# Two inversions half a period apart in a recurrent stage, and their products as 32x32 tiles

## The chip, the cores and the metric

One Trainium2 chip, one of its cores. The metric is device time in microseconds (us) of one execution, lower is better. The kernel before took 2627.87 us (median of 3 runs, 2627.56 to 2632.1).

## The reference, cut to what matters

Two transformer-like layers on one sequence of 1024 tokens, width 1024, all float32: an attention and convolution layer with an MLP, then a hybrid layer whose second half is a recurrent mixer (eight heads of 64). Only that mixer is touched. With a state of 64x64 per head it computes, token by token:

```
def rwkv7_step(state, inp):
    r_t, w_t, k_t, v_t, kk_t, a_t = inp
    sa = jnp.einsum('bhvk,bhk->bhv', state, -kk_t)
    state = (state * w_t[:, :, None, :] + sa[..., None] * (kk_t * a_t)[:, :, None, :]
             + v_t[..., None] * k_t[:, :, None, :])
    y = jnp.einsum('bhvk,bhk->bhv', state, r_t)
    return state, y
...
    _, y = lax.scan(rwkv7_step, s0, (tm(rh), tm(wh), tm(kh), tm(vh), tm(kk), tm(ah)))
```

After it come a group norm over each head, a bonus term, a gate, an output projection of 1024x1024 and a final RMS norm.

## The kernel before, in words

The kernel runs through five phases; the recurrent stage is the first part of the last one (`rwkv_phase`). Each engine has its own instruction stream, written out by hand in a loop over chunks; semaphores order the engines, and within an engine instructions start in program order.

The 1024 tokens are cut into C = 16 chunks of 64. Within a chunk the recurrence is a triangular system per head: u = (I - N)^-1 z, with N strictly triangular of 64x64. Eight heads lie as 4 pairs: head pair m in the free dimension, head e of the pair in partitions 64e to 64e+63. So one product over all heads is 8 matmuls of 64x64 (`pairs`), on two diagonal tiles of the array; a float32 matmul leaves two MATMUL and two LDWEIGHTS records.

For every chunk c:
- ScalarE takes exponentials (`exps`, L2989 to L2991), GpSimd scales the operands (`operands`, L2997 to L3004), TensorE makes the raw scores (`raw`, L3013), VectorE masks them (`masked`, L3026), ScalarE copies the two halves into one tile (`both_heads`, L3031, L3032), GpSimd multiplies it by six level masks (`chunk_levels`, L3038).
- The inverse is built in six levels: level l joins diagonal blocks of 2^l into blocks of 2^(l+1). T and G (the inverse and its transpose) start as identity plus the first mask (L3605, L3609). At each further level TensorE makes X = off_l^T T (`inv_x`), ScalarE copies X out of PSUM (L3479), TensorE makes G^T X and X^T G (`inv_w`), VectorE adds them to T (L3617) and G (L3620). The last level makes the one for G alone. Work is split into two groups of two head pairs, each with PSUM banks and semaphores of its own, so that one group's eviction lies beside the other group's product. All of these products are recorded at L3270.
- Around it: `turn` transposes k and v of the chunk (L3283, L3288; ScalarE evicts, L3465, L3467), `value_part` (L3262) multiplies values with scores (VectorE copies, L3611), `state_part` (L3262) reads the carried state, VectorE adds both (`combine`, L3585), `solve` (L3262) applies G, ScalarE copies u (L3471), `y_part` (L3343, L3347) makes the outputs, `state_product` (L3355) the update, and VectorE's `next_state` (L3590, L3591) forms the next state.

The order on TensorE in iteration c: `state_part(c-1)`, `inv_x(c, 0)`, `turn(c)`, `solve(c-1)`, `inv_x(c, 1)`, `value_part(c)`, `inv_w(c, 1)`, then levels 2 to 5 of chunk c one after the other, with `y_part(c-1)` and `state_product(c-1)` after the second x, `raw(c+1)` after the third. In chunks 8 to 12 sums of the group norm (L3188) are put between, and VectorE and ScalarE do the norm of the first half of the sequence; in chunks 11 to 15 casts for the output projection. After the last chunk TensorE makes 16 output tiles with 24 matmuls each (`project`, L425); tile 0 is made in the last iteration.

Buffers: operands `ra` three deep, scores two deep, level masks two deep; `bkt`, `uv`, `zv` two deep. Weights of the projection are loaded by SyncE into a ring of three slots; all three are full before the stage.

Of the kernel before, what the change touches and what calls it, by code (L numbers as in the profile page):

```python
# [2599 lines left out]
LEVELS = 6  # L2600
GN_EPS = 64e-5
# [10 lines left out]
def gates_phase(k):  # L2612
# [43 lines left out]
    def _(sp):  # L2656
# [19 lines left out]
        load_weights(k, sp, START["wout", 0] + RING)  # L2676
# [282 lines left out]
def chunk_buffers(k):  # L2959
# [12 lines left out]
    b.ra = [x.rearrange("p (c d) -> p c d", c=4) for x in (view_cp(k, 2560), low(0, 4 * P), low(512, 4 * P))]  # L2972
    bk, er, ek = four_of(low(1024, 2, 4 * P)), four_of(low(2048, 2, 4 * CHUNK)), four_of(low(2560, 2, 4 * CHUNK))
    b.bk = lambda c: bk[:, c % 2] if c else early(512, P)
    b.er = lambda c: er[:, c % 2] if c else early(0, CHUNK)
    b.ek = lambda c: ek[:, c % 2] if c else early(256, CHUNK)
    mm, mab = low(3072, 4, 4 * P).rearrange("p (a b) (c d) -> p a b c d", a=2, c=4), four_of(low(5120, 2, 4 * CHUNK))
    free_at = [k.later_pieces.hi_at(k.later_pieces.of_tile[2 * len(IN3_TILES) - 4 + i][0]) for i in range(2)]
    b.mm = lambda c: mm[:, c % 2] if c else four_of(k.data(free_at[0], 2, 4 * P))
    b.mab = lambda c: mab[:, c % 2] if c else four_of(k.data(free_at[1], 1, 4 * CHUNK))[:, 0]  # L2980
    b.off = k.view(XT_AT + 4096, 2 * LEVELS, 4 * CHUNK).rearrange("p (a b) (c d) -> p a b c d", a=2, c=4)
    b.mask, b.level = k.view(CP_AT + CD["mask"][0], P), k.view(CP_AT + CD["level"][0], LEVELS, CHUNK)
    b.last_er, b.er_neg = k.view(CP_AT + 2140, 4, 4), k.data(17408, 4, CHUNK)
# [3 lines left out]
def chunk_exps(k, a, b, c):  # L2987
    at = slice(c * CHUNK, (c + 1) * CHUNK)
    a.activation(b.last_er[:, c % 4], b.L[:, :, (c + 1) * CHUNK - 1], ACT.Exp, scale=-DECAY)  # L2989
    a.activation(b.er(c), b.L[:, :, at], ACT.Exp, scale=-DECAY)  # L2990
    a.activation(b.ek(c), b.L[:, :, at], ACT.Exp, scale=DECAY).then_inc(k.exp_ready, 1)  # L2991


def chunk_operands(k, g, b, c):
    at, o = slice(c * CHUNK, (c + 1) * CHUNK), b.ra[c % 3]
# [12 lines left out]
def chunk_raw(k, pe, b, c):  # L3008
    pe.wait_ge(k.ops_ready, c + 1)
    for m in range(4):  # L3010
        for e in range(2):
            half = slice(64 * e, 64 * e + 64)
            last = pe.matmul(k.bank(e if c else 4 + e).rearrange("p (m c) -> p m c", m=4)[:, m], b.bk(c)[half, m],  # L3013
                             b.ra[c % 3][half, m], start=True, stop=True)
    last.then_inc(k.raw_mm, 1)
# [6 lines left out]
def chunk_masked(k, v, b, c):  # L3022
    v.wait_ge(k.raw_mm, c + 1)
    for e in range(2):
        raw = k.bank(e if c else 4 + e).rearrange("p (m c) -> p m c", m=4)
        v.tensor_tensor(b.mm(c)[:, e], raw, over_pairs(b.mask), ALU.mult).then_inc(k.mm_ready, 1)  # L3026
# [8 lines left out]
def chunk_levels(k, g, b, c, levels=range(LEVELS)):  # L3035
# [5 lines left out]
def rwkv_phase(k):  # L3041
# [22 lines left out]
    mm = chunk.mm  # L3064
    bkt, uv, zv = four_of(low(5632, 2, 4 * P)), four_of(low(6656, 2, 4 * P)), four_of(low(7680, 2, 4 * CHUNK))
    off, tt = chunk.off, four_of(high(3072, 1, 4 * CHUNK))
    gg, zz = four_of(high(3328, 2, 4 * CHUNK)), four_of(high(3840, 1, 4 * CHUNK))
# [15 lines left out]
    x_bank, w_bank, G = (2, 4), (3, 7), (slice(0, 2), slice(2, 4))  # L3083
# [43 lines left out]
    first_split = {(12, 2): 4, (13, 2): 5, (14, 1): 6, (14, 2): 7, (14, 4): 0, (15, 1): 1, (15, 2): 2, (15, 4): 3}  # L3127
# [13 lines left out]
    def half(b, at):  # L3141
        return k.bank(b)[:, at:at + 2 * CHUNK].rearrange("p (m c) -> p m c", m=2)
# [9 lines left out]
    def _(sp):  # L3152
# [17 lines left out]
        sp.wait_ge(y_mm, C)  # L3170
        sp.dma_start(gate[1], part("gate_keep", 1)).then_inc(gate_in[1], 16)
# [12 lines left out]
    def _(pe):  # L3184
# [5 lines left out]
        def mean(i):  # L3190
            if i < 4:
                pe.wait_ge(y_read, 8)
                pe.wait_ge(s_ready, 8 + i)
# [6 lines left out]
        def variance(i):  # L3200
            pe.wait_ge(q2_ready, i + 1)
            if i < 4:
                pe.wait_ge(mm_ready, 2 * (11 + i))
# [61 lines left out]
        def group_pairs(i, bank, at, lhs, rhs):  # L3265

            out = k.bank(bank)[:, at:at + 2 * CHUNK].rearrange("p (m c) -> p m c", m=2)
            for m in range(2):
                for e in range(2):
                    last = pe.matmul(out[rows(e), m], lhs(2 * i + m, e), rhs(2 * i + m, e), start=True, stop=True)  # L3270
            return last

        def raw(c):
            pe.wait_ge(zv_ready, c)
            pe.wait_ge(turn_read, 2 * c)
            chunk_raw(k, pe, chunk, c)

        def turn(c):
            pe.wait_ge(mm_ready, 2 * c + 2)
# [16 lines left out]
        def inv_x(c, l):  # L3296

            pe.wait_ge(off_ready, LEVELS * c + l + 1)
            for i in range(2):
                if l == 0:  # L3300
                    last = group_pairs(i, x_bank[i], 0, lambda m, e: off[rows(e), c % 2, 0, m],
                                       lambda m, e: eye[rows(e)])
                else:
                    pe.wait_ge(t_ready[i], (LEVELS - 1) * c + l)
                    last = group_pairs(i, x_bank[i], 0, lambda m, e: off[rows(e), c % 2, l, m],
                                       lambda m, e: tt[rows(e), 0, m])
                last.then_inc(x_mm[i], 1)

        def inv_w(c, l):

            for i in range(2):
                pe.wait_ge(x_ready[i], (LEVELS - 1) * c + l)
                pe.wait_ge(g_ready[i], LEVELS * c + l)
                if l < LEVELS - 1:
                    group_pairs(i, w_bank[i], 0, lambda m, e: gg[rows(e), c % 2, m],
                                lambda m, e: xx[rows(e), l % 2, m])
                group_pairs(i, w_bank[i], 2 * CHUNK, lambda m, e: xx[rows(e), l % 2, m],
                            lambda m, e: gg[rows(e), c % 2, m]).then_inc(w_mm[i], 1)

        def state_part(c):  # L3320
            if c >= 1:
                pe.wait_ge(s_ready, c)
            if 8 <= c < 12:
                pe.wait_ge(d_ready, c - 7)
            pairs(5, lambda m, e: ra[c % 3][rows(e), m, 64:128], lambda m, e: st[rows(e), 0, m]).then_inc(zs_mm, 1)

        def solve(c):
            pe.wait_ge(z_ready, c + 1)
            for i in range(2):
                pe.wait_ge(g_ready[i], LEVELS * (c + 1))  # L3330
# [6 lines left out]
            pairs(6, lambda m, e: gg[rows(e), c % 2, m], lambda m, e: zz[rows(e), 0, m]).then_inc(u_mm, 1)  # L3337

        def y_part(c):
            pe.wait_ge(u_ready, 2 * c + 2)  # L3340
            for m in range(4):
                for e in range(2):
                    pe.matmul(four(6)[rows(e), m], st[rows(e), 0, m], ra[c % 3][rows(e), m, 0:64], start=m == 0,  # L3343
# [7 lines left out]
        def state_product(c):  # L3351
            pe.wait_ge(z_ready, c + 1)
            for m in range(4):
# [5 lines left out]
        for c in range(C + 1):  # L3359
            if c >= 1:  # L3360
                state_part(c - 1)
            if c < C:
                inv_x(c, 0)
                turn(c)
            else:
                project(0, (0, 4))
            if c >= 1:
                solve(c - 1)
            if c < C:
                inv_x(c, 1)  # L3370
                value_part(c)
                inv_w(c, 1)
            if c == C:
                project(0, (4, KT))
                y_part(c - 1)
            if c < C:
                for l in range(2, LEVELS):
                    inv_x(c, l)
                    if l == 2 and c >= 1:
                        y_part(c - 1)  # L3380
                        state_product(c - 1)
                    if l == 3 and c + 1 < C:
                        raw(c + 1)
                    inv_w(c, l)
                    if l == 3 and 8 <= c < 12:
                        mean(c - 8)
                    if l == 3 and 9 <= c < 13:
                        bonus(c - 9)
                    if l == 4 and 9 <= c < 13:
                        variance(c - 9)  # L3390
        for n in range(1, 16):
            project(n)
# [13 lines left out]
    def _(a):  # L3406
# [37 lines left out]
        def exps(c):  # L3444
            if c >= 2:
                a.wait_ge(ops_ready, c - 1)
            if c >= 4:
                a.wait_ge(s_ready, c - 3)
            chunk_exps(k, a, chunk, c)

        def both_heads(c):

            if c >= 2:
                a.wait_ge(off_ready, LEVELS * (c - 1))
            chunk_heads(k, a, chunk, c)

        cast_at = {(11, 5): 4, (12, 5): 5, (13, 2): 6, (13, 5): 7, (14, 2): 0, (14, 4): 1, (14, 5): 2, (15, 2): 3}
        a.wait_ge(k.in3.filled, 2 * len(IN3_TILES))
        exps(1)
        for c in range(C + 1):  # L3460
            if c < C:
                a.wait_ge(turn_mm, 2 * c + 1)
                if c >= 2:
                    a.wait_ge(y_mm, c - 1)
                a.copy(bkt[:, c % 2], four(0, P)).then_inc(turn_read, 1)  # L3465
                a.wait_ge(turn_mm, 2 * c + 2)
                a.copy(uv[64:128, c % 2], four(1, P)[64:128]).then_inc(turn_read, 1)  # L3467
            if c >= 1:
                a.wait_ge(u_mm, c)
                for e in range(2):  # L3470
                    a.copy(uv[0:64, (c - 1) % 2, :, rows(e)], four(6)[rows(e)]).then_inc(u_ready, 1)  # L3471
            if c < C:
                for l in range(1, LEVELS):
                    n = (LEVELS - 1) * c + l
                    for i in range(2):
                        a.wait_ge(x_mm[i], LEVELS * c + l + 1)
                        if n > 2:
                            a.wait_ge(w_mm[i], n - 2)
                        a.copy(xx[:, l % 2, G[i]], half(x_bank[i], 0)).then_inc(x_ready[i], 1)  # L3479
                    if l == 2 and c == 0:  # L3480
                        k.late_evict()
                    if l == 1 and 11 <= c < 15:
                        pieces.split_ahead(a, 0, most=c - 10)
                    if (c, l) in cast_at:
                        split_hi(0, cast_at[c, l])
                    if l == 3 and c >= 1:
                        a.wait_ge(y_mm, c)
# [376 lines left out]
```

## Time and profile before

| what | value |
|---|---|
| median of 3 runs | 2627.87 us |
| profiled execution, its own time | 2630.19 us |
| span of its instructions | 2628.2 us |
| busy: PE, DVE, ACT, POOL | 98%, 59%, 42%, 16% |
| recurrent stage | about 2255 to 2517 us of the span |

PE is TensorE's matmuls, PEld its weight loads, DVE is VectorE, ACT ScalarE, POOL GpSimd, SP SyncE. A record's span includes its way through the pipeline, so neighbouring records overlap, and the busy time of an engine is that of their union. A timeline row gives start, the time from the first start to the last end, engine, line, operation, operands, shape and number of records, and in brackets the idle time before it and what ended that. In shapes, 64*64 is rows and columns of the array in use, 64x64 output partitions and columns.

### The profile page before, as it was taken

What the parts mean: (1) busy time and instruction counts of PE and PEld (TensorE: products, weight loads), DVE (VectorE), ACT (ScalarE), POOL (GpSimd) and SP (SyncE); (2) the same over time, 40 slices, a digit from 0 to 9 for tenths busy, and PEclk for the clock granted to TensorE, in tenths of its full rate; (3) what the DMA queues carried; (4) which work ended last, traced back from release to release, by engine and by line L of the source; (5) the groups of instructions that cost most, each with busy time, mean ns of one, the idle gap of its engine ahead of it and who ended that gap; (6) DMA issues with size and microseconds to landing.
All of it is one profiled execution on the core that took longest, in us unless ns stands there. A gap on an engine that the chain in (4) does not pass through costs nothing.

```text
span 2628.2 us, 46698 instructions
## 1 busy us (share of the span) xinstructions
PE 2567.8 (98%) x19224; PEld 2086.1 (79%) x19224; DVE 1561.6 (59%) x2521; ACT 1108.6 (42%) x2067; POOL 425.6 (16%) x381
## 2 busy tenths in 40 slices
PE   8999999999999999999999999999999999999998
PEld 6887777778778998899888777766776677788876
DVE  8765443436686665676546676355567646656754
ACT  3242233323355543556335554324445545344521
POOL 4421221100000000000000000111112100456644
PEclk9999999999999999999999999999999999999999
DMA  6753443134423454534534222631011253100032
GB/s 227 212 119 107 97 131 101 65 115 165 160 102 116 144 192 141 189 132 150 170 127 173 76 96 90 270 129 49 29 49 49 85 189 105 42 19 19 19 129 96
DMA packets 80754, 307.24 MB, mean 117 GB/s; under 512 B 7200, under 2 KB 8864, under 8 KB 62624
## 3 DMA queue, kind: packets, MB, share of 16 engines
q1 hardware_dynamic: 55984, 238.72, 25.9%
q0 software_dynamic: 12800, 33.56, 5.6%
q10 hardware_dynamic: 11760, 31.99, 3.2%
q8 instruction: 154, 2.52, 0.4%
q14 instruction: 56, 0.46, 0.1%
HBM read 268.32 MB, written 69.47 MB: 129 GB/s over the span
## 4 chain that ended last, share of the span: by engine, by line
PE 83%; DVE 9%; ACT 4%; issue 3%; DMA 1%; POOL 1%; DVEq 0%; ACTq 0%; SPq 0%; POOLq 0%
PE ps L425 46%; PE ps L3270 4%; PE ps L1258 4%; PE ps L1257 4%; PE ps L1259 4%; PE ps L2145 2%; PE ps L2191 2%; PE ps L2171 2%; PE ps L2072 2%; PE ps L609 2%; PE ps L635 1%; PE ps L2074 1%; PE ps L2073 1%; PE ps L624 1%; DVE parts L404 1%
## 5 line engine op out<-in xcount | busy, mean ns | idle before, releaser
L425 PE MATMUL ps<-parts,parts 128*128 128x512 f32 (+2 forms) x6456 | 1467.5, 387 | 15.9 <-DVE parts L804 8.8
L425 PEld LDWEIGHTS ps<-parts,parts 128*128 128x128 f32 x6456 | 1171.6, 188 | 299.7 <-issue 34.3
L404 DVE TENSOR_TENSOR parts<-ring,parts 128x1024 fp32r<-128x1024 f32 x180 | 220.8, 1238 | 174.7 <-ACT parts L381 166.3
L381 ACT CAST parts<-ring 128x1024 fp32r<-128x1024 f32 x183 | 188.7, 1044 | 116.9 <-DMA ring<-in_weights 62.1
L1257 PE MATMUL ps<-parts,parts 128*128 128x256 f32 x840 | 236.2, 281 | 1.3 <-ACT phase_data L1406 1.3
L1258 PE MATMUL ps<-parts,parts 128*128 128x256 f32 x840 | 236.1, 281 | 0.0
L1259 PE MATMUL ps<-parts,parts 128*128 128x256 f32 x840 | 236.0, 281 | 0.0
L404 POOL TENSOR_TENSOR parts<-ring,parts 128x1024 fp32r<-128x1024 f32 x62 | 153.2, 2472 | 423.1 <-DVE parts L381 423.0
L2552 POOL TENSOR_TENSOR phase_data<-phase_data,stream 128x512 f32<-128x512 f32 x12 | 17.2, 1436 | 1186.2 <-PE ps L2082 1186.2
L867 DVE TENSOR_TENSOR_SCAN stream<-stream 128x513 f32<-128x513 f32 (+3 forms) x96 | 95.2, 992 | 173.2 <-ACT stream L737 173.0
L1257 PEld LDWEIGHTS ps<-parts,parts 128*128 128x128 f32 x840 | 158.7, 189 | 2.4 <-ACT phase_data L1406 1.5
L1258 PEld LDWEIGHTS ps<-parts,parts 128*128 128x128 f32 x840 | 157.7, 188 | 0.8 <-issue 0.5
L1259 PEld LDWEIGHTS ps<-parts,parts 128*128 128x128 f32 x840 | 157.9, 188 | 0.0
L2270 ACT ACTIVATE stream<-stream,phase_data 128x640 f32<-128x640 f32 (+7 forms) x128 | 93.5, 731 | 84.8 <-DVE phase_data L2476 84.2
L1636 DVE TENSOR_TENSOR parts<-phase_data,parts 128x512 fp32r<-128x512 f32 (+1 forms) x111 | 78.1, 730 | 30.2 <-ACT parts L1565 11.0
L1647 DVE TENSOR_TENSOR parts<-ring,parts 128x1024 fp32r<-128x1024 f32 x60 | 72.5, 1220 | 33.1 <-ACT parts L1401 28.3
L3479 ACT COPY phase_data<-ps 128x128 f32<-128x128 f32 x160 | 40.1, 266 | 110.0 <-PE ps L3270 104.2
L2476 DVE CUSTOM_DVE_ANT_0 stream<-ps,phase_scratch 128x640 f32<-128x640 f32 (+4 forms) x96 | 54.4, 598 | 46.7 <-PE ps L2145 45.2
L1401 ACT CAST parts<-ring 128x1024 fp32r<-128x1024 f32 x60 | 63.1, 1051 | 44.3 <-PE ps L425 17.2
L1406 ACT COPY phase_data<-ps 128x256 f32<-128x256 f32 x120 | 44.8, 373 | 87.3 <-PE ps L1259 85.2
L1838 DVE TENSOR_TENSOR phase_data<-phase_data,ps 128x512 f32<-128x512 f32 x48 | 32.9, 686 | 81.8 <-PE ps L425 81.5
L3038 POOL TENSOR_TENSOR stream<-normed,phase_scratch 128x256 f32<-128x256 f32 x90 | 65.6, 763 | 91.1 <-ACT normed L3032 91.1
(391 smaller groups left out, 3761.6 us busy)
## 6 DMA issues: line engine op xcount, KB each, us to landing
ring<-in_weights SPq DMA_DIRECT2D x128, 1024.0 KB, 4.9
up_sums<-in_weights POOLq DMA_DIRECT2D x24, 1024.0 KB, 8.9
ring<-in_weights SPq DMA_DIRECT2D x32, 512.0 KB, 4.3
ring<-up_sums SPq DMA_DIRECT2D x30, 512.0 KB, 5.9
phase_data<-up_sums SPq DMA_DIRECT2D x60, 256.0 KB, 5.6
up_sums<-up_sums POOLq DMA_DIRECT2D x8, 1024.0 KB, 5.4
phase_data<-in_weights SPq DMA_DIRECT2D x30, 256.0 KB, 5.5
raw_keep<-phase_scratch SPq DMA_DIRECT2D x21, 256.0 KB, 2.4
```

The costliest lines, as they stand in the source:

```text
L381: cast(self.hi(p), self.whole(p)).then_inc(self.k.hi_ready, 1)
L404: g.tensor_tensor(self.lo(p), self.whole(p), self.hi(p).bitcast(F32), ALU.subtract).then_inc(self.k.lo_ready, 1)
L425: last = pe.matmul(out, a, b, start=i == 0 and a is ah and b is bh, stop=i == len(pairs) - 1 and a is al)
L867: step(v.tensor_tensor_scan(back, back, back, 1.0, ALU.mult, ALU.min))
L1257: pe.matmul(out, hi, x_hi, start=first and t == 0, stop=False, skip_group_check=True)
L1258: pe.matmul(out, hi, x_lo, start=False, stop=False, skip_group_check=True)
L1259: last = pe.matmul(out, lo, x_hi, start=False, stop=t == 3, skip_group_check=True)
L1636: return v.tensor_tensor(lo, whole_, hi.bitcast(F32), ALU.subtract)
L1647: v.tensor_tensor(quad_lo(r, i), quad_whole(r, i), quad_hi(i).bitcast(F32), ALU.subtract).then_inc(weight_lo.sem, 1)
L2270: a.activation(tile, tile, ACT.Exp, bias=neg_max[:, n:n + 1], scale=-1.0, accum_out=sums[:, n:n + 1]).then_inc(e_ready, 1)
L3038: g.tensor_tensor(b.off[:, c % 2, l], b.mab(c), over_pairs(b.level[:, l]), ALU.mult).then_inc(k.off_ready, 1)
L3270: last = pe.matmul(out[rows(e), m], lhs(2 * i + m, e), rhs(2 * i + m, e), start=True, stop=True)
```

## The change

1. **Overlap.** In iteration c TensorE works on levels 0 to 2 of chunk c, levels 3 to 5 of chunk d = c - 1, and the carried state of chunk e = c - 2. The loop has C + 2 iterations. Groups of head pairs are gone: a product covers all four, and a chunk has the banks and semaphores of its parity. ScalarE, VectorE and GpSimd follow the same order.
2. **Tiles.** Levels 0 to 4 only fill diagonal blocks of 32x32, so from chunk 2 on their products are 16 matmuls of 32x32 on the four diagonal tiles (`blocks`). The first two chunks use 64x64 (`heads`), which also writes the zeros beside the blocks.
3. **Last level.** Level 5 multiplies only the 32x32 corner that it fills, straight from the masked scores, without a mask: five masks per chunk are left.
4. **Buffers.** `ra` is five deep, scores four (`mms`), `bk` and `mab` three, the decays eight. They lie in part in a ring slot of the projection's weights (`lent`), so its third block is loaded after the last `y_part`.
5. **Neighbours.** The norm's sums come two iterations later; the projection's casts are moved; tile 0 is made in the last two iterations, and the first two steps of tile 1 as well.

```diff
+        def heads(out, lhs, rhs):
+            for m in range(4):
                 for e in range(2):
+                    last = pe.matmul(out[rows(e), m], lhs[rows(e), m], rhs[rows(e), m], start=True, stop=True)
             return last
 
+        def blocks(out, lhs, rhs):
+            for m in range(4):
+                for q in range(4):
+                    here, side = slice(32 * q, 32 * q + 32), slice(32 * (q % 2), 32 * (q % 2) + 32)
+                    last = pe.matmul(out[here, m, side], lhs[here, m, side], rhs[here, m, side], start=True, stop=True)
+            return last
+
+        def product(c, out, lhs, rhs):
+            return (blocks if TILED and c >= 2 else heads)(out, lhs, rhs)
...
         def inv_w(c, l):
+            i, n = c % 2, c // 2
+            pe.wait_ge(x_ready[i], TS * n + l)
+            pe.wait_ge(g_ready[i], GS * n + l)
+            if l < LEVELS - 1:
+                product(c, t_out(c), gg(c), xx[:, i])
+                last = product(c, w_out(c, l), xx[:, i], gg(c))
+            else:
+                for m in range(4):
+                    for e in range(2):
+                        upper, lower = slice(64 * e, 64 * e + 32), slice(64 * e + 32, 64 * e + 64)
+                        last = pe.matmul(w_out(c, l)[upper, m, 32:64], xx[lower, i, m, 0:32],
+                                         gg(c)[lower, m, 32:64], start=True, stop=True)
+            last.then_inc(w_mm[i], 1)
...
+        for c in range(C + 2):                       # TensorE
+            d, e = c - 1, c - 2
+            if e >= 0:
+                state_part(e)
+            if 0 <= d < C:
+                turn(d)
             if c < C:
                 inv_x(c, 0)
+            if 0 <= d < C:
+                inv_x(d, 3)
+            if c == C + 1:
+                project(0, (4, KT))
+            if e >= 0:
+                solve(e)
             if c < C:
                 inv_x(c, 1)
+            if 0 <= d < C:
+                inv_w(d, 3)
+                value_part(d)
+            if c < C:
                 inv_w(c, 1)
+            if 0 <= d < C:
+                inv_x(d, 4)
+            if 10 <= c < 14:
+                mean(c - 10)
+            if 0 < c < C - 1:
+                raw(c + 1)
             if c == C:
+                project(0, (0, 4))
+            if 0 <= d < C:
+                inv_w(d, 4)
             if c < C:
+                inv_x(c, 2)
+            if c == C + 1:
+                project(1, (0, 2))
+            if e >= 0:
+                y_part(e)
+            if 0 <= d < C:
+                inv_x(d, 5)
+            if c < C:
+                inv_w(c, 2)
+            if c == 0:
+                raw(1)
+            if 0 <= e < C - 1:
+                state_product(e)
+            if 0 <= d < C:
+                inv_w(d, 5)
+            if 10 <= c < 14:
+                variance(c - 10)
+                bonus(c - 10)
...
+        for c in range(C + 2):                       # VectorE
+            d, e = c - 1, c - 2
+            if 11 <= c < 15:
+                take_bonus(c - 11)
             if c < C:
+                open_inverse(c)
+            if e >= 0:
+                combine(e)
+            if 0 <= d < C:
+                add_t(d, 3)
+                add_g(d, 3)
+                v.wait_ge(zv_mm, d + 1)
+                v.tensor_copy(zv[:, d % 2], four(0)).then_inc(zv_ready, 1)
+            if c < C:
+                add_t(c, 1)
+                add_g(c, 1)
...
+            if 0 < c < C - 1:
+                masked(c + 1, (0,))
+            if 0 <= d < C:
+                add_t(d, 4)
+            if 0 < c < C - 1:
+                masked(c + 1, (1,))
+            if 0 <= d < C:
+                add_g(d, 4)
+            if c < C:
+                add_t(c, 2)
+                add_g(c, 2)
...
+            if 0 <= e < C - 1:
+                next_state(e)
+            if 0 <= d < C:
+                add_g(d, 5)
...
+        levels(0, range(1, 3))                       # GpSimd
+        operands(1)
+        levels(0, range(3, MASKS))
+        levels(1, range(2))
+        operands(2)
+        levels(1, range(2, MASKS))
+        operands(3)
+        for c in range(2, C):
+            levels(c, range(MASKS))
+            if c + 2 < C:
+                operands(c + 2)
```

On ScalarE the order of an iteration is: copy k turned, `copy_x(d, 3)`, copy v turned, `copy_x(c, 1)`, the two copies of u(e), `copy_x(d, 4)`, `exps(c + 3)`, `copy_x(c, 2)`, `copy_x(d, 5)`, `both_heads(c + 1)`, the copy of y(e).

## Rows read from the trace of the kernel before

**Rows 1.** The page: busy time by engine, the chain by engine, the instruction queue.
```profile
PE 2567.8 (98%) x19224; PEld 2086.1 (79%) x19224; DVE 1561.6 (59%) x2521; ACT 1108.6 (42%) x2067; POOL 425.6 (16%) x381
PE 83%; DVE 9%; ACT 4%; issue 3%; DMA 1%; POOL 1%; DVEq 0%; ACTq 0%; SPq 0%; POOLq 0%
q8 instruction: 154, 2.52, 0.4%
```
**Rows 2.** Busy time by stretch of the stage; columns in the first row.
```profile
core 0: us, PE busy (x) PEld busy (x) DVE busy (x) ACT busy (x) POOL busy (x), PEclk, DMA share, GB/s
2268.00:2390.00 122.00, 117.37 (x2880) 104.16 (x2882) 68.34 (x224) 50.10 (x162) 69.86 (x100) 1.00 0.04 12
```
**Rows 3.** Instructions of line 3585: ns least/median/most, first and last start.
```profile
L3585 DVE TENSOR_TENSOR stream<-ps,normed x16: 424/425/425, 2270.2 to 2509.5; 128x256 f32<-128x256 f32 x16
```
**Rows 4.** Timeline of TensorE, one chunk and the start of the next.
```profile
2330.61 0.63 PE L3270 MATMUL ps<-phase_scratch,stream 64*64 64x64 f32 x16
2331.17 0.66 PE L3283 MATMUL ps<-constants,normed 128*128 128x128 f32 x4
...
2332.19 0.68 PE L3262 MATMUL ps<-stream 64*64 64x64 f32 x16
...
2336.56 0.69 PE L3347 MATMUL ps<-normed 128*64 128x64 f32 x16
...
2339.56 1.16 PE L3013 MATMUL ps<-phase_scratch,normed 64*128 64x128 f32 x16
...
2345.77 0.63 PE L3270 MATMUL ps<-phase_scratch,stream 64*64 64x64 f32 x16
```
**Rows 5.** Timeline in windows of 15 ns at 2330.605 and 2330.665; spans of single records.
```profile
2330.61 0.23 PE L3270 MATMUL ps<-phase_scratch,stream 64*64 64x64 f32 x2
...
2330.61 0.28 PE L3270 MATMUL ps<-phase_scratch,stream 64*64 64x64 f32 x4
...
L3270 PE MATMUL ps<-stream x1280: 218/218/267, 2257.4 to 2508.0; 64*64 64x64 f32 x183
...
L3013 PE MATMUL ps<-normed 64*128 64x128 f32 x160 | 11.6, 284 | 0.5 <-POOL normed L3004 0.5
```
**Rows 6.** VectorE and ScalarE: timeline rows, and line 3605's least, median and most.
```profile
2331.86 0.58 ACT L3465 COPY normed<-ps 128x512 f32<-128x512 f32 x1 [2.09 <-PE ps L3283]
2333.08 0.76 ACT L3471 COPY normed<-ps 64x256 f32<-64x256 f32 x2
2339.24 0.41 DVE L3590 TENSOR_TENSOR phase_data<-phase_data,ps 128x256 f32<-128x256 f32 x1
2339.69 0.42 DVE L3591 TENSOR_TENSOR phase_data<-phase_data,phase_scratch 128x256 f32<-128x256 f32 x1
2342.25 1.28 DVE L3026 TENSOR_TENSOR normed<-ps,phase_scratch 128x512 f32<-128x512 f32 x2
2345.98 0.42 DVE L3585 TENSOR_TENSOR stream<-ps,normed 128x256 f32<-128x256 f32 x1 [0.18 <-PE ps L3262]
...
L3605 DVE TENSOR_TENSOR stream<-stream,phase_scratch x32: 281/808/862, 2255.6 to 2495.0; 128x128 f32<-128x128 f32 x32
...
2502.89 1.27 POOL L3671 TENSOR_TENSOR phase_data<-phase_data 128x512 f32<-128x512 f32 x1
2502.94 1.50 DVE L3591 TENSOR_TENSOR phase_data<-phase_data,phase_scratch 128x256 f32<-128x256 f32 x1
```
**Rows 7.** Timeline: the stage's first product, one chunk of GpSimd, the second output tile.
```profile
2255.51 0.68 PE L3270 MATMUL ps<-phase_scratch,stream 64*64 64x64 f32 x16 [0.17 <-POOL stream L3038]
...
2329.45 4.26 POOL L3038 TENSOR_TENSOR stream<-normed,phase_scratch 128x256 f32<-128x256 f32 x6 [7.04 <-ACT normed L3032]
2333.67 0.72 POOL L2997 TENSOR_TENSOR phase_scratch<-phase_data,normed 128x256 f32<-128x256 f32 x1
...
2336.85 0.73 POOL L3004 TENSOR_TENSOR normed<-phase_data,normed 128x256 f32<-128x256 f32 x1
...
2517.18 5.84 PE L425 MATMUL ps<-parts,parts 128*128 128x512 f32 x24
```
**Rows 8.** DMA queues between 2260 and 2500: packets, MB, share of 16 engines.
```profile
q8 instruction: 43, 0.70, 1.2%
```

More of the change, by code:

```diff
@@ L3342, in y_part @@
                 for e in range(2):
-                    pe.matmul(four(6)[rows(e), m], st[rows(e), 0, m], ra[c % 3][rows(e), m, 0:64], start=m == 0,
+                    pe.matmul(four(6)[rows(e), m], st[rows(e), 0, m], ra[c % 5][rows(e), m, 0:64], start=m == 0,
                               stop=False, skip_group_check=True)
@@ L3458, in _ @@
         a.wait_ge(k.in3.filled, 2 * len(IN3_TILES))
         exps(1)
-        for c in range(C + 1):
-            if c < C:
[L3462 to L3471, printed above, removed]
-            if c < C:
[L3473 to L3487, printed above, removed]
-                        a.copy(A[:, :, at(c - 1)], four(6)).then_inc(y_read, 1)
-                    if l == 2 and c + 2 < C:
-                        exps(c + 2)
-                    if l == 4 and c + 1 < C:
-                        both_heads(c + 1)
-                if 8 <= c < 12:
-                    square(c - 8)
-                if 9 <= c < 13:
-                    inverse_root(c - 9)
-            else:
-                a.wait_ge(y_mm, c)
-                a.copy(A[:, :, at(c - 1)], four(6)).then_inc(y_read, 1)
@@ new lines, in _ @@
+        exps(2)
+        for c in range(C + 2):
+            d, e = c - 1, c - 2
+            if 0 <= d < C:
+                a.wait_ge(turn_mm, 2 * d + 1)
+                if d >= 2:
+                    a.wait_ge(s_mm, d - 1)
+                a.copy(bkt[:, d % 2], four(0, P)).then_inc(turn_read, 1)
+                copy_x(d, 3)
+                a.wait_ge(turn_mm, 2 * d + 2)
+                a.copy(uv[64:128, d % 2], four(1, P)[64:128]).then_inc(turn_read, 1)
+            if c < C:
+                copy_x(c, 1)
+            if e >= 0:
+                a.wait_ge(u_mm, e + 1)
+                for h in range(2):
+                    a.copy(uv[0:64, e % 2, :, rows(h)], four(6)[rows(h)]).then_inc(u_ready, 1)
+            if 0 <= d < C:
+                copy_x(d, 4)
+            if c == C:
+                split_hi(0, 7)
+            if c + 3 < C:
+                exps(c + 3)
+            if 12 <= c < 15:
+                pieces.split_ahead(a, 0, most=c - 11)
+            if c < C:
+                copy_x(c, 2)
+            if c == 0:
+                k.late_evict()
+            if 0 <= d < C:
+                copy_x(d, 5)
+            if 10 <= c < 14:
+                square(c - 10)
+            if c + 1 < C:
+                both_heads(c + 1)
+            if e >= 0:
+                a.wait_ge(y_mm, e + 1)
+                a.copy(A[:, :, at(e)], four(6)).then_inc(y_read, 1)
+            if 10 <= c < 14:
+                inverse_root(c - 10)
+            if 13 <= c < C:
+                split_hi(0, c - 9)
+            if c == C:
+                for t in range(4):
+                    split_hi(0, t)
@@ L3636, in _, with masked, open_inverse @@
-        v.wait_ge(k.hi_ready, pieces.base + 4)
+        def masked(c, es):
+            if c >= 5:
+                v.wait_ge(y_mm, c - 3)
+            chunk_masked(k, v, chunk, c, es)
+        def open_inverse(c):
+            i, n = c % 2, c // 2
+            v.wait_ge(off_ready, MASKS * c + 1)
+            if c >= 3:
+                v.wait_ge(u_mm, c - 2)
+            v.tensor_tensor(gg(c), off[:, i, 0], bc(eye), ALU.add).then_inc(g_ready[i], 1)
+            v.wait_ge(x_mm[i], XS * n + 1)
+            v.tensor_tensor(tt[:, i], x_out(c, 0), bc(eye), ALU.add).then_inc(t_ready[i], 1)
@@ new lines, in add_t, with add_g @@
+        def add_t(c, l):
+            i, n = c % 2, c // 2
+            v.wait_ge(w_mm[i], WS * n + l)
+            v.wait_ge(t_ready[i], TS * n + l)
+            v.tensor_tensor(tt[:, i], tt[:, i], t_out(c), ALU.add).then_inc(t_ready[i], 1)
+        def add_g(c, l):
+            i, n = c % 2, c // 2
+            v.wait_ge(w_mm[i], WS * n + l)
+            v.wait_ge(g_ready[i], GS * n + l)
+            if l < LEVELS - 1:
+                v.tensor_tensor(gg(c), gg(c), w_out(c, l), ALU.add).then_inc(g_ready[i], 1)
+            else:
+                for h in range(2):
+                    x = gg(c)[64 * h:64 * h + 32, :, 32:64]
+                    last = v.tensor_tensor(x, x, w_out(c, l)[64 * h:64 * h + 32, :, 32:64], ALU.add)
+                last.then_inc(g_ready[i], 1)
@@ L3660, in operands, with levels @@
         def operands(c):
-            if c >= 3:
-                g.wait_ge(y_mm, c - 2)
-            if c >= 2:
-                g.wait_ge(turn_read, 2 * c - 3)
+            if c >= 5:
+                g.wait_ge(y_mm, c - 4)
+            if c >= 4:
+                g.wait_ge(turn_read, 2 * (c - 3) + 1)
             chunk_operands(k, g, chunk, c)
+        def levels(c, which):
+            if c >= 2 and which[0] == 0:
+                g.wait_ge(x_mm[c % 2], XS * (c // 2 - 1) + MASKS)
+            chunk_levels(k, g, chunk, c, which)
         rk = k.const("r_k_2")
```

241 lines of the change are left out of this document (108 added, 133 removed).

## The prediction

> **What bounds the kernel now.** Read first: the page. TensorE is busy 98% of the span and the chain that ended last is TensorE for 83% [rows 1]. The change lies in the recurrent stage alone, so next come the stretches of that stage: PE is busy 96% there too, but DVE only 56%, ACT 41% and POOL 57% in its first half, at full clock [rows 2]. A busy PE is not a PE at its peak, so the stage is read by its period and its starts. DVE's combine L3585 runs once per chunk, from 2270.2 to 2509.5 [rows 3]; one undisturbed chunk takes 2345.77 - 2330.61 = 15.16 us [rows 4]. Fifteen periods would be 227.4; they take 239.3, so layer-norm sums and casts in the later chunks cost 11.9 more. The stage runs from the first product at 2255.51 to the second output tile at 2517.18 [rows 7]: 261.7 us.
>
> What fills the 15.16? A product of 16 records (8 fp32 matmuls of 64x64, two records each) spans 0.63; take off one record's 0.218 and the first pair's offset and seven steps remain: 0.058 a pair. Two records start at almost the same time (two reach 0.23, four 0.28) [rows 5]; the tiles of one pair run side by side, and a product takes 8 x 0.058 = 0.47. The raw scores have 128 columns: (1.16 - 0.28 - 0.10 for its start) / 7 = 0.111 a pair [rows 4, 5]. So 64 columns cost 0.053, and 0.005 stays whatever their number. Changing the tile shape costs more: the last 64x64 record starts at 2330.61 + 0.63 - 0.22 = 2331.02, the first transpose at 2331.17, 0.15 in place of 0.058, and the weight load after it isn't ahead either: L3347 spans 0.69 where L3270 spans 0.63 [rows 4], 0.05 more. So 0.14 a change of shape. Sum of a chunk now: 15 inversion products 7.0; state, solve, value, two for y, state product 6 x 0.47 = 2.8; raw scores 0.9 (L3013: 1.16 less 0.27); 8 transposes 0.9 (L3283 to L3262, less the change); six changes 0.84. That is 12.4; the other 2.7 are waits of the chain product, eviction, product.
>
> **The change part by part.** *Products as 32x32 tiles.* Thirteen products a chunk (levels 0 to 4) become 16 matmuls of 32x32, 32 records in eight sets of four diagonal tiles. The trace has no such shape. Lower end: the second of a pair starts within about 10 ns of the first and the array needs half of 53 = 27 ns for 32 columns, plus the 5: 32 ns a set, 0.25 a product. Upper end: each record costs what it costs on average now, 0.47 / 16 = 29 ns: 0.94. Even 14.7 ns a record gives 0.47, nothing won. I take 0.25: the row of the pairs [rows 5] shows records starting almost together when their tiles are apart, so 29 ns is array time shared by two and not a cost of a record. *Level 5* becomes two products of 16 small records, two side by side: 0.25 each, 0.5.
>
> *More changes of shape.* In the new order state, turn, x0/x3, solve, x1/w3, value, w1/x4, raw, w4/x2, y (two shapes), x5/w2, state product, w5 there are 14: 14 x 0.14 = 2.0 (between 0, if 32 and 64 rows don't clash, and 3). PE's sum: 13 x 0.25 + 0.5 + 2.8 + 0.9 + 0.9 + 2.0 = 10.4 us a chunk (before 12.4).
>
> *The waits.* Two inversions alternate, so most evictions are covered: between x1(c) and w1(c) now stand w3(d) and value(d), 1.1 us, against ACT's copy of 0.38. I laid one period out from the start of state_part. State ends 0.47, turns 1.5, x0 1.9, x3 2.15. DVE's open_inverse waits for x0's end (2.1), 0.42 for T, then combine 0.42 [rows 6] with handovers of 0.05: z at 3.0, while PE is ready for solve at 2.3. A wait of **0.75**. Then x1, w3, value, w1, x4, raw, w4, x2, y, x5, w2 find their inputs done; w2 is issued by 10.1, w5 by 11.1. The next state_part needs next_state, behind add_t and add_g of w2 on DVE: 10.35 + 2 x 0.4 + 0.45 + the second step. That step is 0.42 alone but reads and writes SBUF alone, and such operations slow down beside POOL: L3605 takes 281 ns or 862, L3591 once 1.50 beside L3671 [rows 6]. POOL starts the next chunk's masks right then; I take 0.6. State starts at 12.3: **1.1** waited. Period: 10.4 + 0.75 + 1.1 = **12.3 us**. Bounds: 11.2 (switches half price, no POOL clash) to 13.8 (sets at 45 ns, the pair's 52 after the last of four, less what waits swallow).
>
> *DVE, ACT, POOL.* DVE: one 256-wide opening (0.4 alone, 1.3 beside POOL), T, combine, copy, eight adds at 0.38, level 5 0.45, masks 1.28, next state 1.1: 8.3 us, fits. ACT: 2 x 0.58 + 2 x 0.38 + 5 x 0.37 + exps 1.0 + heads 0.8 + y 0.38: 6. POOL: five masks instead of six, 3.6, and 3.9 of operands [rows 7]: 7.5. The first mask of the next chunk is done about 11.9 (raw 7.3, masked 8.95, heads 11.1), product x0 wants it at 1.6 of the next period. Larger buffers for operands and masks are what lets raw(c+1) be early; they cost nothing. One ring slot is lent, so one 1 MB block is loaded after the last y; it is wanted four output tiles (23 us) later and takes 5: hidden.
>
> *Instruction fetch.* Queue q8 brings 2.52 MB for 2 x 19224 records and loads, 66 bytes each, in packets of 16 KB (250 of them); 43 packets in 240 us at 1.2% of 16 engines are 1.07 us each [rows 1, 8]. The new chunk has 1136 records and loads, 4.5 packets, 4.9 us of 12.3. It holds on average.
>
> *Ends of the stage.* Chunks 0 and 1 aren't tiled and not overlapped: from x0(0) to turn(0) 9.4 us (the chain to w2 6.7; then raw(1), masked, heads; chunk 1's operands end about 2260.8), then 11.1 to state_part(0), then 1.1 until POOL, which does operands 2 and 3 first, has chunk 2's first mask: 21.6. Fourteen full periods: 172.2. Later extras as now: 11.9 (the same three sums a chunk). Two closing iterations with projections inside: 10.2 + 7.3, less 1.5 for the two steps of tile 1 done ahead: 16.0. Together 221.7 against 261.7: **40.0 saved**. The stretch behind it (2517 on) is PE-bound and keeps its work. The profiled execution took 2630.2 around a span of 2628.2; 2590.2 by its measure, and as it stood 2.3 over the median of the runs, **2588** on theirs.
>
> **A rule that speaks against it.** The Trainium skill, "TensorE: Matmul & The Clock Gate", section "Back-to-back issue gap", gives small matmuls a floor of about 25 ns from start to start however few the columns. The rows show less than that inside a pair [rows 5], 58 ns only for the same tile. If it held for each record, an estimate by that page would be 32 x 25 = 0.8 a product. The same page, "Packing small matmuls", has about 4 ns between tiles, which the pairs favour.
>
> **The rivals.** In general the saving is 212.2 less 14 periods.
> - *Records have a price of their own* (the other side). Place: the 13 tiled products. Up to 14.8 ns a record a chunk comes to 15.2 and nothing is lost; beyond it the change is slower. At 29 ns: 10.4 + 13 x 0.69 + 1.85 = 21.2, 85 slower, 2713; at a third of the way (19 ns, 0.61) 17.0, 26 slower. For it: twice the instructions, none of the shape seen, queue fetch in bursts. Against: the pairs. Chance 0.12.
> - *Tiles bring nothing, overlap does*: 0.47 a product, period 15.1, 2627. Also what comes out if tile writes into one PSUM bank go two at a time. 0.06.
> - *DVE and the order become the bound.* With POOL busy most of a shorter period, the opening and next state at their slow values (1.3 and 1.5), and finish, centre, bonus and split (4.4 a chunk) for chunks 11 to 13 on top of 8.3: DVE 12.7 of work, plus its in-order waits. Period 13.8 to 14.5, 2609 to 2619. For it: L3605's 862, against it: DVE has 4 us free in a plain period. 0.17.
> - *Better than forecast*: changes to 32x32 free, T behind x0 early; period 10.8, 2567. 0.10.
>
> **How the numbers follow.** Forecast 0.55 (2572 to 2609 around 2588), the rest as above. Range for 8 in 10: 2564 to 2619, which leaves out most of the first two rivals and the far end of the better one. A measurement here tells 0.2% (5.3 us) from none. Faster: 0.55 + 0.17 + 0.10 and a little = 0.83; same 0.06; slower 0.11.
>
> **What would show it.** Right: 32x32 records in sets of four, 32 ns a set; combine L3585's successor every 12.3 us in plain chunks; PE waiting for DVE before solve and before state; 14 steps of 0.15 a chunk. Wrong: sets over 60 ns (rival one or two); DVE busy over 85% and PE waiting on it in more than two places (rival three); a clock under full because PE pauses in the first two chunks; or PE waiting for POOL's masks.

## The result and the profile after

The changed kernel took 2669.53 us (median of 4 runs, 2667.73 to 2676.23), the kernel before 2628.77 beside it: ratio 1.0157, 95% interval 1.0145 to 1.0169. It is 1.6% slower; the forecast was 2588, and the range ended at 2619. The profiled execution is the slowest of the four, 2676.23 around a span of 2674.4.

The recurrent stage alone accounts for it. First the busy time of a stretch inside it, after and then before:

```profile
core 0: us, PE busy (x) PEld busy (x) DVE busy (x) ACT busy (x) POOL busy (x), PEclk, DMA share, GB/s
2300.00:2500.00 200.00, 161.59 (x6050) 135.55 (x6048) 89.48 (x206) 63.60 (x166) 93.61 (x122) 0.78 0.05 15
```
```profile
2300.00:2500.00 200.00, 191.91 (x4502) 164.39 (x4500) 126.06 (x378) 91.01 (x269) 127.43 (x164) 1.00 0.06 19
```

PE is idle 19% of the time instead of 4%, though it issues a third more records, and every other engine has less to do per microsecond. The granted clock, 1.00 before [rows 2], is 0.78: it goes back and forth between its two levels, 2.4 and 1.2 GHz. So two things could be the cause, PE's idle time for want of something and the low clock, and this stretch shows both.

The stage begins with the first product at 2256.94 and ends where the projection runs on, at 2564.32. Less the 1.6 us of tile 1 done ahead that is 305.8 us, against 261.7 before [rows 7]: 44 of the 46 us between the two profiled executions. VectorE's `combine` gives the period, [rows 3]:

```profile
L3662 DVE TENSOR_TENSOR stream<-ps,normed x16: 407/414/425, 2282.4 to 2559.7; 128x256 f32<-128x256 f32 x16
...
2337.18 0.41 DVE L3662 TENSOR_TENSOR stream<-ps,normed 128x256 f32<-128x256 f32 x1
2354.47 0.41 DVE L3662 TENSOR_TENSOR stream<-ps,normed 128x256 f32<-128x256 f32 x1
...
2408.12 0.42 DVE L3662 TENSOR_TENSOR stream<-ps,normed 128x256 f32<-128x256 f32 x1
2426.71 0.41 DVE L3662 TENSOR_TENSOR stream<-ps,normed 128x256 f32<-128x256 f32 x1
```

17.3 and 18.6 us a chunk, where 12.3 was forecast and 15.16 was the time before. From the first `combine` to the fifteenth 263.3 us pass (2282.4 to 2545.7); the forecast had 14 x 12.3 and 11.9 for the extras of the later chunks, 184.1. That is 79 of the 84 us by which the stage missed its forecast (221.7). The same two periods as stretches, clock in the third column from the right:

```profile
2337.18:2354.47 17.29, 15.04 (x572) 13.83 (x568) 7.29 (x19) 5.50 (x16) 6.29 (x9) 0.66 0.02 5
2408.12:2426.71 18.59, 13.98 (x568) 12.09 (x568) 7.06 (x20) 5.40 (x15) 11.16 (x16) 0.83 0.02 4
```

The period with the lower clock is the shorter one. What PE does inside the second is in its timeline (start, span, records, and in brackets the idle time and what ended it); "issue" means that it waited for nothing that the profile shows:

```profile
2408.59 0.68 PE L3285 MATMUL ps<-stream 64*64 64x64 f32 x16 [0.59 <-DVE stream L3662]
2409.20 0.45 PE L3300 MATMUL ps<-stream 32*32 32x32 f32 x32
...
2410.84 0.26 PE L3300 MATMUL ps<-stream,phase_data 32*32 32x32 f32 x6 [0.64 <-issue]
2411.03 0.68 PE L3285 MATMUL ps<-normed,phase_data 64*64 64x64 f32 x16
2411.64 0.45 PE L3300 MATMUL ps<-phase_data,stream 32*32 32x32 f32 x32
2411.91 0.48 PE L3300 MATMUL ps<-stream,phase_data 32*32 32x32 f32 x32
2412.25 0.45 PE L3300 MATMUL ps<-stream 32*32 32x32 f32 x32
2412.63 0.71 PE L3022 MATMUL ps<-phase_scratch,normed 64*128 64x128 f32 x8
2415.02 0.72 PE L3022 MATMUL ps<-phase_scratch,normed 64*128 64x128 f32 x8 [1.68 <-issue]
2415.67 0.45 PE L3300 MATMUL ps<-phase_data,stream 32*32 32x32 f32 x32
2415.94 0.48 PE L3300 MATMUL ps<-stream,phase_data 32*32 32x32 f32 x32
2416.28 0.45 PE L3300 MATMUL ps<-stream 32*32 32x32 f32 x32
2416.66 0.68 PE L3387 MATMUL ps<-normed,phase_data 64*64 64x64 f32 x16
2417.27 0.45 PE L3391 MATMUL ps<-ring,normed 128*64 128x64 f32 x7
2418.97 0.46 PE L3391 MATMUL ps<-ring,normed 128*64 128x64 f32 x9 [1.26 <-issue]
```

The tiles are as fast as forecast: a product of 32 records spans 0.45, less the 0.19 of one record 0.26 (forecast 0.25). But PE stops in the middle of a product, 8 records into the raw scores and 7 into `y_part`. From one stop to the next it runs 6 + 16 + 32 + 32 + 32 + 8 = 126 matmuls and then 8 + 96 + 16 + 7 = 127, with as many weight loads: 252 and 254 records, one packet of the instruction queue [rows 8]. PE starts again 4.2 and 3.95 us after it last did. For the tiles alone the idle time before them adds up to this in the whole stage (us, times):

```profile
  issue: 47.5, 67
```

The Trainium skill, "Advanced Engine Details and Errata", section "ISA Cache", says that the instruction cache is held in lines of 16 KB, 256 instructions. The packets and the distance of the stops agree with it.

The trace has the start of every packet of the instruction queue too. The last packets before these three restarts (2410.84, 2415.02, 2418.97) start at 2408.48, 2412.74 and 2416.50, 2.3 to 2.5 us ahead of them. It is so in the whole stage: between 2285 and 2560 PE stops 26 times for over 0.6 us from one record to the next of the same product (the norm's sums left out), and each time it goes on 2.2 to 2.8 us after a packet has started.

### The profile page after: what moved, and what is told of

It is laid out like the page before. It is cut to its first block, busy times and chain, and to the rows that moved or that the text cites. A ratio compares the mean times of both kernels' runs of the same rounds, so it can differ in the third digit from the quotient of the medians.

```text
span 2674.4 us, 52095 instructions
## 1 busy us (share of the span) xinstructions
PE 2565.1 (96%) x22136; PEld 2080.6 (78%) x22136; DVE 1547.8 (58%) x2364; ACT 1096.5 (41%) x1986; POOL 418.5 (16%) x365
## 4 chain that ended last, share of the span: by engine, by line
PE 82%; DVE 9%; issue 4%; ACT 3%; DMA 1%; POOL 1%; DVEq 0%; SPq 0%; ACTq 0%; POOLq 0%
PE ps L425 44%; PE ps L1258 4%; PE ps L1257 4%; PE ps L1259 4%; PE ps L3300 3%; PE ps L2145 2%; PE ps L2191 2%; PE ps L2171 2%; PE ps L2072 2%; PE ps L609 2%; PE ps L635 1%; PE ps L3285 1%; PE ps L2074 1%; PE ps L2073 1%; PE ps L624 1%
## 5 line engine op out<-in xcount | busy, mean ns | idle before, releaser
L3528 ACT COPY phase_data<-ps 128x256 f32<-128x256 f32 x80 | 29.7, 372 | 148.9 <-PE ps L3300 103.6
L3690 DVE TENSOR_TENSOR stream<-stream,ps 128x256 f32<-128x256 f32 x64 | 27.0, 421 | 102.7 <-PE ps L3300 90.4
L1406 ACT COPY phase_data<-ps 128x256 f32<-128x256 f32 x120 | 44.7, 373 | 87.4 <-PE ps L1259 85.4
```

## The experiments

Theory F: PE runs out of instructions. Theory G: the clock gate, fed by short tiles, sets the time. The times of e3, e4 and e5 are medians of two executions each, those of the others of four to ten.

**e1, the overlap without the tiles:** `TILED = False`.

> The changed kernel with all products of levels 0 to 4 as 64x64 matmuls (TILED = False): the overlap without the tiles, 360 matmul records a chunk instead of 568. Theory F (instruction fetch): queue q8 brings 256 instructions in 3.5 to 3.9 us at best; in the changed kernel PE stalls 0.6 to 1.9 us every 253 records, so 568 records and 568 loads need 4.5 packets x 3.75 = 16.8 us a chunk whatever the array does. With 360 the fetch needs 10.7 and no longer binds; PE's work and waits do: period 15.1, total 2620 to 2632, clock near full. Theory G (clock gate: the short tiles give the array too little to do, the clock falls to half, and PE at half clock sets the period): the clock is full again, the same total. The run gives what the overlap alone is worth; both theories fail if it stays at 2660 or more.

Measured: 2633.87, ratio 1.0013 (1.0004 to 1.0023), clock 0.995. The plain period, from `combine` to `combine`:

```profile
2338.61 0.41 DVE L3662 TENSOR_TENSOR stream<-ps,normed 128x256 f32<-128x256 f32 x1
2352.88 0.41 DVE L3662 TENSOR_TENSOR stream<-ps,normed 128x256 f32<-128x256 f32 x1
```

14.27: better by 0.9 than before. Filling the pipeline costs it back, for the first `combine` comes at 2281.6, 11.4 later than before [rows 3], and so does VectorE in the later chunks (e6). Of the changed kernel's 1.6% all but 0.1% came with the tiles. The expected total (2620 to 2632) was missed by 2.

**e2, tiles in six products of thirteen,** those of levels 1 to 3 in `inv_w`:

```
-                product(c, t_out(c), gg(c), xx[:, i])
-                last = product(c, w_out(c, l), xx[:, i], gg(c))
+                product(c, t_out(c), gg(c), xx[:, i], l < 4)
+                last = product(c, w_out(c, l), xx[:, i], gg(c), l < 4)
```

> Overlap, with 32x32 tiles in 6 of the 13 products only (the two of levels 1 to 3 in inv_w), 456 records a chunk. Theory F: fetch 3.6 packets x 3.75 = 13.5 us, PE 10.4 + 7 x 0.22 + 1.85 = 13.8: both about balanced, total 2605 to 2622, faster than with all tiles by 50 and than with none by some 10. Theory G: half of the tiles, so part of the clock is lost: between e1 and the changed kernel, 2635 to 2655.

Measured: 2639.15, ratio 1.0034 (1.0021 to 1.0047). A miss for F as it was put, and inside G's numbers: tiles in half of the products don't give half of the gain but cost 5 us against e1, though the average rate of packets would allow it. Its periods vary from 14.3 to 17.6. Its trace speaks against G all the same. PE stops in the middle of a product at full clock (first row; the clock is third from the right), and only afterwards does the clock fall to half (second row):

```profile
2309.60:2329.80 20.20, 15.79 (x610) 14.13 (x606) 10.00 (x25) 7.29 (x20) 10.97 (x16) 1.00 0.17 56
2330.00:2333.30 3.30, 3.30 (x38) 2.85 (x36) 0.51 (x2) 0.59 (x1) 1.13 (x4) 0.50 0.00 0
```
```profile
2325.32 0.31 PE L3300 MATMUL ps<-stream,phase_data 32*32 32x32 f32 x12
2327.40 0.37 PE L3300 MATMUL ps<-stream,phase_data 32*32 32x32 f32 x19 [1.78 <-issue]
```

It left open how much of the time is the clock's (e4) and whether a packet is judged by itself (e8, e9).

**e4, as many records as with the tiles, but the array as busy as without.** Four matmuls side by side, each with all 64 rows and 64 moving columns, and 32 of the stationary ones:

```
-                    last = pe.matmul(out[here, m, side], lhs[here, m, side], rhs[here, m, side], start=True, stop=True)
+                    last = pe.matmul(out[here, m], lhs[rows(q // 2), m, side], rhs[rows(q // 2), m], start=True, stop=True)
```

> Overlap; each of the 13 products that the changed kernel tiles is done on the full 64 rows and 64 columns of moving data, but with the 64 stationary columns in two matmuls of 32: four side by side for 53 ns instead of two, so the array is held as long as by 64x64 products, with as many records (568) as with the tiles. Theory F: fetch binds as in the changed kernel, total 2655 to 2680, stalls every 253 records. Theory G: array as busy as in e1, clock full, total as e1 (2620 to 2632).

Measured: 2676.56, ratio 1.0175 (1.0155 to 1.0196), with the clock at 0.97 in the stretch where the changed kernel had 0.78:

```profile
2300.00:2500.00 200.00, 164.69 (x6141) 137.96 (x6131) 89.69 (x208) 64.77 (x168) 95.19 (x126) 0.97 0.05 15
```

The stops are there as well (idle time before the split products, us and times):

```profile
  issue: 40.8, 58
```

The loss is there whole, almost without the low clock. G falls as its cause. In the chunks before the norm's sums (first `combine` to eighth) the period is 17.6 on average, against 18.0 in the changed kernel.

**e5, the same split in the kernel before,** without overlap or tiles:

```
-                for e in range(2):
-                    last = pe.matmul(out[rows(e), m], lhs(2 * i + m, e), rhs(2 * i + m, e), start=True, stop=True)
+                for q in range(4):
+                    here, side = slice(32 * q, 32 * q + 32), slice(32 * (q % 2), 32 * (q % 2) + 32)
+                    last = pe.matmul(out[here, m], lhs(2 * i + m, q // 2)[:, side], rhs(2 * i + m, q // 2), start=True, stop=True)
```

> The kernel before, no overlap and no tiles, every product of the inversion with its stationary 64 columns in two matmuls of 32: the same array time, 600 matmul records a chunk instead of 360. Theory F: 4.74 packets x 3.75 = 17.8 us a chunk instead of 15.16, total about 2668 (2655 to 2680). Theory G: no change of what the array does, 2625 to 2640.

Measured: 2678.6, ratio 1.0183 (1.0163 to 1.0204), 48 us slower by nothing but the number of records, at full clock. PE stops in the middle of products here too:

```profile
2342.21 0.28 PE L3271 MATMUL ps<-phase_data,stream 64*32 64x64 f32 x4
2343.90 0.36 PE L3271 MATMUL ps<-phase_data,stream 64*32 64x64 f32 x10 [1.42 <-issue]
```

The stretch, and its instruction queue:

```profile
2300.00:2500.00 200.00, 176.35 (x6415) 139.48 (x6408) 108.20 (x324) 75.44 (x228) 104.10 (x139) 1.00 0.05 15
...
q8 instruction: 51, 0.84, 1.8%
```

51 packets, one every 3.9 us. The same row of before, of the changed kernel, and of e7 (below):

```profile
q8 instruction: 36, 0.59, 1.3%
```
```profile
q8 instruction: 47, 0.77, 1.6%
```
```profile
q8 instruction: 43, 0.70, 1.5%
```

A packet is on its way for some 1.1 us in all of them (1.8% x 16 x 200 / 51), so the time on its way does not set the rate. PE used a packet every 5.6 us before. On average over these 200 us no run got one oftener than every 3.9; the closest two packets of any run start 3.3 us apart. What makes up these 3.3 to 3.9 us stays open. The traces show only the order: after a stop in the middle of a product PE goes on 2.2 to 3.0 us after a packet's start, and the next packet starts 1.1 us or more after that.

**e3, the tiled products for two of four head pairs** (the others are left out): `for m in range(2)` in `blocks`.

> The changed kernel with the tiled products computed for two of the four head pairs only (half of the tiles left out, the rest of the work kept): short 32x32 products in the same places, but 360 matmul records a chunk as in e1. Theory F (instruction fetch): 2.85 packets x 3.8 = 10.8 us, PE's work 8.8 plus about 1.1 of waits; period 11 to 12, total 2585 to 2610. Theory G (clock gate sets the time): the array has still less to do, the clock stays at half for much of the stage, PE at half clock needs 14.7 and the total is 2635 or more.

Measured: 2603.28, ratio 0.99 (0.9882 to 0.9918). Periods 11.0 to 12.5 in the plain chunks, for instance:

```profile
2333.13 0.41 DVE L3662 TENSOR_TENSOR stream<-ps,normed 128x256 f32<-128x256 f32 x1
2344.98 0.41 DVE L3662 TENSOR_TENSOR stream<-ps,normed 128x256 f32<-128x256 f32 x1
2356.20 0.41 DVE L3662 TENSOR_TENSOR stream<-ps,normed 128x256 f32<-128x256 f32 x1
```

Short tiles are fine when there are few enough of them. The clock was 0.91 between 2300 and 2500, so it was not full here either.

**e6, e1 with VectorE's extra work moved.** In e1 PE idled 3.5 us for `combine` in chunk 12, behind `split_lo`, `take_bonus` and a slow opening on VectorE:

```profile
2459.53 1.22 DVE L3632 TENSOR_TENSOR parts<-phase_data,parts 128x512 fp32r<-128x512 f32 x1
2460.77 0.69 DVE L3610 TENSOR_TENSOR phase_data<-ps,phase_data 128x512 f32<-128x512 f32 x1
2461.50 2.41 DVE L3682 TENSOR_TENSOR stream<-stream,phase_scratch 128x256 f32<-128x256 f32 x1
...
2464.17 0.41 DVE L3662 TENSOR_TENSOR stream<-ps,normed 128x256 f32<-128x256 f32 x1
...
2464.63 1.12 PE L3285 MATMUL ps<-stream 64*64 64x64 f32 x16 [3.49 <-DVE stream L3662]
```

```
                 v.tensor_copy(zv[:, d % 2], four(0)).then_inc(zv_ready, 1)
+            if 14 <= c <= C:
+                split_lo(0, c - 10)
...
-                finish(c - 11, (1, 2))
+                finish(c - 11)
...
-            if 11 <= c < 15:
-                finish(c - 11, (3, 4))
-            if 13 <= c < C:
-                split_lo(0, c - 9)
```

> e1 with VectorE's extra work of the later chunks moved: finish() whole in the middle of the iteration, where VectorE waits for the raw scores, and split_lo() of tiles 4 to 6 one iteration later, behind the copy of zv. In e1 they stand ahead of combine, and PE idles 3.5 and 4.0 us for it in chunks 12 and 13. Theory F and the reading of e1: those two periods fall from 19.2 to 16.5, 5 to 9 us off, total 2624 to 2629. Rival: VectorE is full there and the same work delays the next wait instead: 2631 to 2635.

Measured: 2622.86, ratio 0.9974 (0.9965 to 0.9984), 1 us under the range. The two long periods are 16.8 and 14.7 now (19.3 and 19.2 in e1).

**e7, e6 with tiles in three products,** `inv_x` of level 0 and both of `inv_w`'s level 2.

> e6 with 32x32 tiles in three of the thirteen products, those that lie ahead of PE's two waits for VectorE: level 0 of inv_x (before combine and solve) and the two of level 2 of inv_w (before next_state). 408 records a chunk: fetch 3.23 packets x 3.75 = 12.1 us, PE 13.2 - 0.65 + 1.06 = 13.6. Theory F, if a packet's slack is there: 14 x 0.6 = 9 less than e6, 2615 to 2621. If a packet that is used up in under 3.75 us stalls whatever the others leave, as e2 suggests, half of it or less: 2620 to 2632.

Measured: 2613.42, ratio 0.9937 (0.9924 to 0.9949): 0.6% faster than the kernel before, the best version that computes everything. Its plain period:

```profile
2337.56 0.41 DVE L3662 TENSOR_TENSOR stream<-ps,normed 128x256 f32<-128x256 f32 x1
2350.94 0.41 DVE L3662 TENSOR_TENSOR stream<-ps,normed 128x256 f32<-128x256 f32 x1
```

13.38, where 13.6 was expected; the total is 1.6 us under F's range. So the packets with tiles had the slack here, and PE never stops for long in the middle of a product.

**e8 and e9, two more tiled products** (`l in (2, 4)` and `l in (1, 2)` in place of `l == 2` in `inv_w`).

> e7 with 32x32 tiles in the two products of level 4 as well, which follow the raw scores (1.0 us for 32 records and loads, slow to use a packet up). 440 matmul records a chunk. By the average, fetch needs 3.48 packets x 3.75 = 13.0 us and PE 12.9: period 13.1, total 2606 to 2611. By the packet (one used up in under 3.75 us stalls, whatever the others leave): some stalls, period 13.2 to 14, total 2609 to 2622.

> e7 with the two products of level 1 as tiles in place of level 4: they stand in the densest part (between value_part and x4), with the same 440 records a chunk as e8. By the average the same as e8 (2606 to 2611). By the packet: more stalls than e8, period 13.5 to 14.5, total 2614 to 2628.

Measured: e8 2617.83, ratio 0.9946 (0.993 to 0.9963); e9 2621.13, ratio 0.9967 (0.9954 to 0.998). Neither beats e7, and both fit "by the packet" and lie above the range of the average. With 3.9 us a packet, as e5 has it, in place of the 3.75 expected, the average alone would give 13.5 us for the 880 records and loads of a chunk, and 14.0 for e2's 912. From the first `combine` to the ninth the periods average 13.4 in e7, 14.05 in e8, 14.4 in e9 and 15.6 in e2. So time is lost beyond the average, clearly in e2 and e9. In e8 it is less clear: its profiled execution is the slowest of four (2612.78 to 2620.47). That e9 is the worse one fits as well, but the two intervals overlap.

**All runs side by side.** Stops are those of over 0.6 us in the middle of a product, between 2285 and 2560, without the norm's sums; packets are those of the instruction queue between 2300 and 2500.

| run | stops | packets | clock, 2300 to 2500 | ratio to before |
|---|---|---|---|---|
| before | 0 | 36 | 1.00 | 1 |
| e1 | 0 | 37 | 0.98 | 1.0013 |
| e6 | 0 | 38 | 1.00 | 0.9974 |
| e7 | 0 | 43 | 1.00 | 0.9937 |
| e8 | 4 | 47 | 0.98 | 0.9946 |
| e3 (half of the tiles left out) | 6 | 39 | 0.91 | 0.99 |
| e9 | 8 | 46 | 0.98 | 0.9967 |
| e2 | 14 | 45 | 0.95 | 1.0034 |
| changed kernel | 26 | 47 | 0.78 | 1.0157 |
| e4 | 30 | 48 | 0.97 | 1.0175 |
| e5 | 28 | 51 | 1.00 | 1.0183 |

Each of these stops, in every run, ends 2.2 to 3.0 us after a packet has started. The three that lose most, the changed kernel, e4 and e5, have 26 to 30 of them and clocks of 0.78, 0.97 and 1.00.

## Why the prediction was wrong

- **The step that failed** is "Instruction fetch": "It holds on average." It took the 1.07 us that a packet is on its way for the price of a packet, set 4.9 us against 12.3 and gave fetch nothing in the sum. The price is the time from one packet to the next, 3.9 us on average at best (e5), and 4.5 packets x 3.9 = 17.5 us a chunk. The periods in plain chunks were 16.5 to 20.2, 18.0 on average. And an average doesn't decide: a packet that PE uses up sooner stalls it, and slow ones don't pay that back in full (e2, e9). "Queue fetch in bursts" stood among the reasons for the first rival, which had 0.12. Its form, a price for each record, is about what happened: 3.9 us for 127 matmuls is 31 ns each, on average. But it took the chain's waits on top (21.2 us a period) where they lie under the stalls, and so came to 2713.
- **The tiles' array time was right:** 0.26 a product (forecast 0.25), four side by side. So were the price of a change of shape (0.61 from `solve` to the tiles of x1 in the timeline above, 0.47 + 0.14) and, roughly, the places where PE waits for VectorE: 0.59 before that `solve` (0.75 forecast), 0.70 before the `state_part` ahead of it (1.1). The argument from the pairs [rows 5] was sound for the array and said nothing of supply. 64x64 products back to back use 32 records in 0.47 us, 254 in 3.7: that is already less than 3.9, and only its waits and slower instructions kept the kernel before clear. The 3.7 could have been read from [rows 4] and the 66 bytes a record; the 3.9 could not, for PE never stopped there for over 0.6 us in the middle of a product.
- **The overlap was rated too low:** period 14.27 in e1, where the sum with 64x64 products was 15.1 (13.2 of work and 1.85 of waits; 1.1 were left). With fetch out of the way the method holds: e7 13.38 for 13.6 expected, e3 11 to 12.5 for 11 to 12.
- **The first chunks** cost little more than forecast: `turn` of chunk 0 starts 9.4 after the first product, as said, and its `state_part` 13.5 after that, where 11.1 was put and 1.1 for a wait for GpSimd that does not come. That is 22.9 for 21.6.
- **VectorE in the late chunks** was a rival at 0.17. Alone it was not the bound, but its order cost e1 some 10 us (1.0013 against 0.9974 of the kernel before), as e6 shows.
- **The clock** was taken as full in the sum. It fell where short tiles and stops came together, in e2 right behind a stop; with the same stops and longer matmuls it stayed at 0.97 (e4) and 1.00 (e5). In plain chunks the period at 0.66 was no longer than that at 0.83. In the later ones it does cost something: the records of the norm's sums start 0.85 us apart at half clock (around 2465) and 0.43 apart at full clock (around 2443). How much that adds was not measured by itself; e4, with most of the low clock gone, was no faster.
- **The rule on small matmuls** (the Trainium skill, "TensorE: Matmul & The Clock Gate", section "Back-to-back issue gap": about 25 ns from start to start) does not hold for tiles side by side: 32 records start within 0.26 us, 8 ns apart on average. The 0.8 a product by that rule was three times too high.

## What to carry to other kernels

Before cutting matmuls into smaller ones, count instructions by the packet: add up the time in which PE would run each 127 fp32 matmul records and their weight loads. Where that was under about 3.9 us PE stalled here, with "issue" as the releaser and 252 to 254 records from stop to stop as the sign. Small tiles paid where they stood before a wait, so that their packet had time to spare, and a few in the right place (e7) beat all of them. When two things go wrong together, as clock and stalls did here, split them with a kernel that has one and not the other.

## What was not expected of the hardware

- The instruction supply of TensorE was never faster than 51 packets of 16 KB in 200 us (e5), 3.9 us each, though each is on its way for 1.1. The stops come every 252 to 254 matmul and weight-load records, and end 2.2 to 3.0 us after a packet's start.
- The granted clock was 0.78 where short tiles and stops of 1.3 to 1.7 us came together. With such stops but longer matmuls it was 0.97 (e4) and 1.00 (e5).
- A VectorE operation on SBUF alone, 128x256, took 2.41 us while GpSimd was at work (e1, line 3682); the slowest of this size in the rows before was 1.50 [rows 6].
